# Reordering ScalarE's and VectorE's work in a two-layer hybrid mixer backbone

## What is computed

```python
for l in range(DEPTH):
    mod = jnp.split((silu_c @ w_mod[l] + b_mod[l])[:, None, :], 6, axis=-1)
    u = modulate(rmsnorm(h, g_mix_pre[l]), mod[0], mod[1])
    # y = (sum over 4 branches of sigmoid(gates_i) * (branch_i(u) @ w_branch[i])) @ w_out
    #     branches: a windowed attention, b bidirectional mLSTM, c latent attention, d differential attention
    y, y_ctx = token_mixers(u, uc, w_in[l], ...)
    h = h + mod[2] * rmsnorm(y, g_mix_post[l])
    u = modulate(rmsnorm(h, g_ffn_pre[l]), mod[3], mod[4])
    h = h + mod[5] * rmsnorm(swiglu(u, w_gate_up[l], w_down[l]), g_ffn_post[l])
    # the context stream hc likewise, in the first layer
return h
```

## Time and profile before

| what | value |
|---|---|
| median of three runs | 3376.95 us (3375.93 to 3379.35) |
| the profiled execution's own time | 3375.98 us |
| its span, first to last instruction | 3374.2 us |
| mean granted clock of TensorE | 0.977 |
| HBM read, written | 273.9 MB, 33.3 MB |

### The profile page before, as it was taken

How to read it: one execution, slowest core, us unless ns; L and a number is a source line. 1 busy time by engine, 2 the same in 40 slices (tenths; PEclk the granted TensorE clock), 3 DMA queues, 4 the chain that set the end, 5 groups by cost and what they waited for, 6 DMA issues and landing times. The chain is left out here.

```text
span 3374.2 us, 47244 instructions
## 1 busy us (share of the span) xinstructions
PE 3200.8 (95%) x18520; PEld 2902.2 (86%) x18520; DVE 1713.8 (51%) x3183; ACT 1136.5 (34%) x1931; POOL 216.7 (6%) x170
## 2 busy tenths in 40 slices
PE   7999989999999989899999989999999999899998
PEld 4999988998899879899999988877787887788886
DVE  6644465424346865764222575545433578553334
ACT  3233234423322544312222432334433225432323
POOL 0001100100021011000000000010100110100000
PEclk9999999999999999899999989999999999999999
DMA  5511230221052023432222443141221421332333
GB/s 204 171 38 59 87 124 26 76 91 45 23 187 76 26 75 121 135 125 68 70 63 59 136 144 103 63 125 38 88 88 38 167 77 38 138 113 84 109 88 93
DMA packets 356826, 310.27 MB, mean 92 GB/s; under 512 B 40527, under 2 KB 335389, under 8 KB 355229
## 3 DMA queue, kind: packets, MB, share of 16 engines
q1 hardware_dynamic: 334478, 240.65, 23.0%
q10 hardware_dynamic: 22158, 67.03, 5.3%
HBM read 273.94 MB, written 33.29 MB: 91 GB/s over the span
## 5 line engine op out<-in xcount | busy, mean ns | idle before, releaser
L868 PE MATMUL ps<-u_hi,w_hi 128*128 128x384 f32 (+1 forms) x2080 | 604.7, 353 | 22.3 <-DVE u_lo L2439 8.5
L868 PE MATMUL ps<-u_lo,w_hi 128*128 128x384 f32 (+1 forms) x2080 | 598.8, 350 | 0.0
L868 PE MATMUL ps<-u_hi,w_lo 128*128 128x384 f32 (+1 forms) x2080 | 598.7, 350 | 0.0
L2051 DVE TENSOR_TENSOR w_lo<-w_raw,w_hi 128x2048 fp32r<-128x2048 f32 x129 | 297.2, 2304 | 345.7 <-ACT w_hi L1520 343.8
L868 PEld LDWEIGHTS ps<-u_hi,w_hi 128*128 128x128 f32 x2080 | 380.4, 190 | 45.9 <-issue 24.8
L868 PEld LDWEIGHTS ps<-u_hi,w_lo 128*128 128x128 f32 x2080 | 383.3, 190 | 19.2
L868 PEld LDWEIGHTS ps<-u_lo,w_hi 128*128 128x128 f32 x2080 | 383.6, 190 | 18.8
L1520 ACT ACTIVATE w_hi<-w_raw 128x2048 fp32r<-128x2048 f32 x129 | 246.1, 1908 | 213.8 <-issue 91.2
L1238 PE MATMUL ps<-u_hi,w_hi 128*128 128x384 f32 (+1 forms) x816 | 310.3, 380 | 4.5 <-ACT space L1818 3.5
L1238 PE MATMUL ps<-u_hi,w_lo 128*128 128x384 f32 (+1 forms) x816 | 296.0, 363 | 0.0
L1238 PE MATMUL ps<-u_lo,w_hi 128*128 128x384 f32 (+1 forms) x816 | 293.5, 360 | 0.0
(11 more groups left out here) (305 smaller groups left out, 5241.2 us busy)
## 6 DMA issues: line engine op xcount, KB each, us to landing
w_raw<-in_w_in SPq DMA_DIRECT2D x288, 256.0 KB, 4.0
space<-in_w_mod SPq DMA_DIRECT2D x48, 1024.0 KB, 5.2
w_raw<-in_w_gate_up SPq DMA_DIRECT2D x176, 256.0 KB, 3.7
w_raw<-in_w_down SPq DMA_DIRECT2D x114, 192.0 KB, 2.7
w_raw<-in_w_branch SPq DMA_DIRECT2D x64, 256.0 KB, 3.5
w_raw<-in_w_out SPq DMA_DIRECT2D x48, 256.0 KB, 3.6
m_scratch<-space ACTq DMA_DIRECT2D x3, 3072.0 KB, 10.2
space<-m_scratch ACTq DMA_DIRECT2D x3, 3072.0 KB, 10.6
```

Of the source, the lines that this page charges most:

```text
L868: last = nc.tensor.matmul(ps[:, 2 * (t % 2) + b, 0:a1 - a0], wv[w][:, k, j * P:(j + 1) * P], xx[:, k, a0:a1], start=(k == 0 and w == 0 and ...
L2051: V.tensor_tensor(w_lo[slot][:, :], w_raw[slot][:, :], w_hi[slot][:, :].bitcast(F32), ALU.subtract).then_inc(w_lo_done, 1)
```

## The change

It moves work and adds little. ScalarE copies three high parts of branch3 between the two units of weights. In the mLSTM preparation TensorE's cumulative sums go from behind tile 5 to behind tile 6, ScalarE's exponential and logarithm from tile 3 to tile 4. VectorE multiplies the first two output-gate tiles ahead of the weight split. At a seam's end the weight split goes ahead of the mean. A one-element Silu is added at the end of the two seams before up0. In the tail the residual comes back in one transfer, is turned by 128 tokens x 8 chunks after the last product, into the eight PSUM banks, and the output operation reads it there; the 8 copies by VectorE fall away, the first sums go ahead of the last three products, and the stores read contiguous rows. The three units at a_q go elsewhere: the first layer's d_q, then up0, take the next ones, the last three of the second layer ride behind units 3, 6 and 9 of its up0 (`sparse`); up0 is written out in both layers (`unrolled`).

```diff
 class Background:
+        self.sparse = False
+    def at(self, i):
+        unit = self.first + i
+        return (self.layer, unit) if unit < MOD_UNITS else (self.layer + 1, unit - MOD_UNITS)
     def behind(self, at):
+        if self.sparse:
+            return [at // 3 - 1] if at % 3 == 0 and 0 < at // 3 <= self.end - self.first else []
...
-    for at, name, l, first, end, tile in ((0, "misc", 0, 8, 15, 4), (0, "a_q", 0, 15, 18, 24), (0, "d_q", 0, 18, 24, 20),
-                                          (0, "up0", 1, 0, 11, 0), (1, "misc", 1, 11, 18, 4), (1, "d_q", 1, 18, 24, 20)):
+    for at, name, l, first, end, tile in ((0, "misc", 0, 8, 15, 4), (0, "d_q", 0, 15, 21, 20), (0, "up0", 0, 21, 32, 0),
+                                          (1, "misc", 1, 8, 15, 4), (1, "d_q", 1, 15, 21, 20),
+                                          (1, "up0", 1, 21, 24, 0)):
         background[starts[at, name]] = Background(l, first, end, 1, b0, tile)
+        for g in groups:
+            background[starts[at, name]].sparse = end - first <= sum(h.n for h in groups) // 3
+            g.unrolled = end > MOD_UNITS or end - first < sum(h.n for h in groups) - 1
@@ pairs
-    first = whole if g.name in SQUARED else 1 if peel or g.early else 0
+    first = whole if g.name in SQUARED or g.unrolled else 1 if peel or g.early else 0
@@ SyncE
-                             H_TOKEN[:, :, token_tile(t)]).then_inc(out_stored, 16)
+                sp.dma_start(out[0, t * P:(t + 1) * P, :], out_tile(t)).then_inc(out_stored, 16)
@@ TensorE, gemm_unit in down1 of the second layer
-                                if made and k == HALF // 2:
-                                    turn_h(made - 1)
                                 if made and k == HALF // 2 + 1:
                                     turn_y(made - 1)
-                                if made == KD - 1 and k == HALF - 1:
+                                if made == KD - 1 and k == HALF - 2:
                                     final_sums(False)
@@ TensorE, prepare_b
-                if made == 5:
+                if made == 6:
                     pe.wait_ge(lf_ready, l + 1)
@@ TensorE, gemm, behind the last product
-                    turn_h(KD - 1)
+                    turn_h(groups[-1], 0)
                     final_sums(True)
                     turn_y(KD - 1)
+                    for t in range(1, SEQ // P):
+                        turn_h(groups[-1], t)
+            def turn_h(g, t):
+                if t == 0:
+                    pe.wait_ge(h_back, 16)
+                if t == 1:
+                    made = g.t0 + KD - 1
+                    pe.wait_ge(acc_free[made % 2], made // 2 + 1)
+                if t == 2:
+                    pe.wait_ge(mean_ready, n.mean)
+                if t == 3:
+                    pe.wait_ge(y_token, KD)
+                for k in range(KD):
+                    at = k * P % BW
+                    last = nc.tensor.transpose(ps[:, 2 * t + k * P // BW, at:at + P], H_LAST[:, k, token_tile(t)],
+                                               ident[:, :])
                 last.then_inc(h_turned, 1)
@@ ScalarE, prepare_b
-                if made == 3:
+                if made == 4:
                     act.wait_ge(lf_abs, DEPTH + l + 1)
@@ ScalarE, gemm
-                    act.dma_start(space[:, 0:8, CTX], h_dram[:, :, CTX_LEN:CTX_LEN + CTX_LEN]).then_inc(h_back, 16)
-                    act.dma_start(H_LATE, h_dram[:, :, 2 * CTX_LEN:TOK]).then_inc(h_back, 16)
+                    act.dma_start(H_LAST, h_dram[:, :, LAT]).then_inc(h_back, 16)
+                    if g.name == "branch3":
+                        gemm_unit(g, 0, 0)
+                        merged_high(g, 0, 3)
+                        gemm_unit(g, 0, 1)
+                        continue
...
+                    merged_high(g, 3, KD - 1)
+                    split_unit(following, 1, None)
+                    merged_high(g, KD - 1, KD)
@@ ScalarE, close
+                if following.kind == "swiglu":
+                    own.did(A(warm[:, :], half_neg[:, :], ACT.Silu))
+                    own.wait()
@@ VectorE, gemm_unit
+                if g.name == "gates1_rest":
+                    output_gate(g.layer, 0, 2)
                 if not first or not (g.early or g.name.startswith("down")):
                     split(g, it, s)
...
-                        output_gate(g.layer, g.lat)
+                        output_gate(g.layer, 2, NT)
+                        output_low(g.layer, g.lat)
...
-                        if k:
-                            h_copy(k - 1)
@@ VectorE, close
+                split(following, 0, 0)
                 part_mean(g, 1, h_sums, 2 * e + 2, next_mean)
-                split(following, 0, 0)
@@ VectorE, finish_output
-                h_copy(KD - 1)
...
                 for i in range(SEQ // P):
+                    dve.wait_ge(h_turned, i + 1)
+                    V.scalar_tensor_tensor(out_tile(i).rearrange("p (k n) -> p k n", k=KD), Y_TOKEN[:, :, token_tile(i)],
                                            root[:, CT + i:CT + i + 1],
-                                           H_TOKEN[:, :, token_tile(i)], ALU.mult,
+                                           ps[:, 2 * i:2 * i + 2, :].rearrange("p b (k n) -> p (b k) n", n=P), ALU.mult,
                                            ALU.add).then_inc(out_made, 1)
```

More of the change, by code:

```diff
@@ L72, in __init__ @@
         self.x, self.kind, self.dst = x, kind, dst
-        self.last = self.early = False
+        self.last = self.early = self.unrolled = False
         self.halves = 1 if lat else 2
@@ L97, in __init__, with stretches @@
         self.layer, self.first, self.end, self.per, self.b0, self.tile = layer, first, end, per, b0, tile
+        self.sparse = False
+    def at(self, i):
+        unit = self.first + i
+        return (self.layer, unit) if unit < MOD_UNITS else (self.layer + 1, unit - MOD_UNITS)
+    def stretches(self):
+        if self.end <= MOD_UNITS:
+            return [(self.layer, self.first, self.end)]
+        return [(self.layer, self.first, MOD_UNITS), (self.layer + 1, 0, self.end - MOD_UNITS)]
     def behind(self, at):
+        if self.sparse:
+            return [at // 3 - 1] if at % 3 == 0 and 0 < at // 3 <= self.end - self.first else []
         return [i for i in range(self.per * at, self.per * (at + 1)) if i < self.end - self.first]
     def rest(self, weight_units):
+        if self.sparse:
+            return range(0)
         return range(min(self.per * weight_units, self.end - self.first), self.end - self.first)
@@ L682, in load_back @@
                 slot = (bk.b0 + i) % 2
+                if isinstance(it, int):
+                    layer, unit = bk.at(i + 2 * bk.per * it)
+                    at = unit * 256
+                else:
+                    layer, at = bk.layer, (bk.first + i) * 256 + it * bk.per * 512
                 sp.dma_start(back_raw(bk, slot).rearrange("p (k n) -> p k n", k=KD),
-                             mod_cols(bk.layer, (bk.first + i) * 256 + it * bk.per * 512)).then_inc(
-                                 back_landed[slot], 16)
+                             mod_cols(layer, at)).then_inc(back_landed[slot], 16)
             def load_unit(g, it, s):
@@ L798, in unit @@
                             load_unit(g, it, s)
-                        if bk is not None and isinstance(it, int) and g.u0 - groups[0].u0 + s + 2 * it == 1:
+                        if bk is not None and isinstance(it, int) and g.u0 - groups[0].u0 + s + 2 * it == (3 if bk.sparse else 1):
                             sp.wait_ge(others_end, 3 * index)
@@ L856, in back_unit @@
                 pe.wait_ge(back_summed, bk.b0 + i + 1 + 2 * bk.per * it)
+                at = 4 * bk.at(i + 2 * bk.per * it)[1] if isinstance(it, int) else 4 * (bk.first + i) + 8 * bk.per * it
                 for j in range(2):
[L858 removed]
+                    last = part_product(back_part(bk, (bk.b0 + i) % 2), j, at)
                 last.then_inc(back_used, 1)
@@ L1141, in gemm @@
                 if groups[-1].name in SQUARED:
-                    turn_h(KD - 1)
+                    turn_h(groups[-1], 0)
                     final_sums(True)
                     turn_y(KD - 1)
-            def turn_h(k):
-                if not k:
-                    pe.wait_ge(h_back, 32)
-                if k:
-                    pe.wait_ge(h_token, k)
-                for t in range(SEQ // P):
-                    src = space[:, k, token_tile(t)] if t < CT else H_LATE[:, k, token_tile(t - CT)]
-                    last = nc.tensor.transpose(ps[:, 5, token_tile(t)], src, ident[:, :])
+                    for t in range(1, SEQ // P):
[14 more added lines that the diff above has]
+                                               ident[:, :])
                 last.then_inc(h_turned, 1)
@@ L1627, in y_copy, with merged_high @@
                 A(Y_TOKEN[:, k, :], ps[:, 6, :], ACT.Copy).then_inc(y_token, 1)
+            def merged_high(g, first, end):
```

(18 more changed lines are left out.)

20 lines of the change are left out of this document (9 added, 11 removed).

## The result

The changed kernel took 3344.49 us in the median (3343.54 to 3346.87, four runs), the kernel before 3378.15 on the same chip: ratio 0.9893, 95% interval 0.988 to 0.9907, so 1.07% faster, where I forecast 1.7%. 3344.5 lies above my range (3306 to 3342). Run once more, beside the kernel before at 3380.55, it took 3339.99: ratio 0.9888 (0.9862 to 0.9914). The profiled execution took 3345.4 us, its span is 3343.7, its mean granted clock 0.979 (before 0.977).

What follows compares the result with a forecast made beforehand. TensorE, busy 95% of the span, was taken as the bound, so only its stalls and the low clock behind them count. Seven terms summed to 55.9 us, 18.8 of it clock: 3376.0 to 3320 us, 1.7% faster, range 3306 to 3342.

Steps and rivals of the forecast that it cites:

- a_q: First layer: modulation units leave this phase; 8.9 plus 0.6 of clock, less 2.7 in second-layer up0, net 6.8 us.
- mLSTM preparation: Later cumulative sums remove the log-gate waits and low clock: 3.4 us in the first layer, 5.7 in the second, together 9.1.
- Output gate: Two multiplies ahead of the w_lo split remove the third turn's waits and low clock: 4.5 + 6.1 = 10.6 us.
- branch1's first unit, over 10 us off: Output gate: what the delayed w_lo split holds up is wanted only there, more than 10 us later.
- branch3: Early high parts on ScalarE remove accumulator waits and low clock, less a new 1.4 us wait: 6.5 + 4.3 = 10.8.
- Norms: Three seams: splitting w_lo ahead of the mean shortens TensorE's wait for GpSimd's root; 5.8 us, no clock gain.
- Silu table: Start of up0, both layers: dummy activation hides the 1.28 us load and the clock stays up; 6.0 us.
- My sign of being wrong: A w_lo split or chunk sum as releaser in branch3 or up0, output operations over 1.3 us, or clock falling as often.
- Tail: End of down1: residual turns leave, its transfer wait and low clock go, first sums cost 1.0; 6.8 us gained.
- (a): Rival: stalls go but the clock does not come back, 3339 us; chance 0.15, half of it lying in between.
- (b): Rival: VectorE becomes the pace in branch3 and in up0's three units, 3330 us; chance 0.12.
- the likeliest case: All seven terms hold, giving 3320 us; chance 0.59.

Runs made afterwards that it cites:

- e8: Changed kernel with the 4-byte tile warm allocated behind all other tiles instead of ahead of the large ones; 3334.65 us, ratio 0.9854.
- e9: Kernel before with one unused 4-byte tile, moving the large tiles by 32 bytes; 3389.66 us, ratio 1.0027.
- e4: Changed kernel with the mLSTM preparation put back, cumulative sums, exponential and logarithm one tile earlier; 3351.34 us, ratio 0.9919.
- e13: e11 with the output gate as before, all multiplies behind VectorE's w_lo split; 3333.14 us, 6.1 over e11.
- e1: Changed kernel with the chunk sums behind the gate product in the first unit of the first layer's up0; 3331.55 us, ratio 0.9856.
- e2: Changed kernel without the dummy Silu that loads the table early; 3335.40 us, ratio 0.9868.
- e7: Kernel before with only the dummy Silu added at the end of the seams that lead into up0; 3389.47 us, ratio 1.0023.
- e16: Kernel before with one unused tile of 256 bytes, moving the large tiles by 256 bytes; 3380.42 us, ratio 0.9995.
- e0: The changed kernel run and profiled once more, nothing altered; 3339.99 us, ratio 0.9888.
- e11: Changed kernel with three repairs: warm behind all tiles, late chunk sums in first-layer up0, residual's load after the third tile; 3327.02 us, ratio 0.9838.
- e6: Changed kernel with late chunk sums in first-layer up0 and the residual's load after the third tile, warm not moved; 3329.50 us, ratio 0.9848.
- e3: Changed kernel with the residual's load in the seams behind w_out issued after the third tile instead of the seventh; 3333.52 us, ratio 0.9867.
- e10: Kernel before with one unused tile of 64 bytes, moving the large tiles by 64 bytes; 3385.69 us, ratio 1.0012.
- e15: Kernel before with one unused tile of 128 bytes, moving the large tiles by 128 bytes; 3385.91 us, ratio 1.0021.

## Why the prediction was off, point by point

**What bounds the kernel: right.** TensorE's busy time didn't move (3200.8 to 3199.2), and all gain came from its waits and its clock.

**a_q: right as a term.** 9.4, 8.8 for a sum of 9.5, and 2.7 for the units in up0 of the second layer (-1.1 is the 2.7 less the 1.7 of clock that I had booked there). The wait in front of prep_a is 1.73 instead of 3.55, and the clock behind is 0.54 for 0.61, so that it fell as far behind the shorter stall:

```profile
458.98 0.44 PE L1255 MATMUL ps<-ident,space 128*128 128x128 f32 x2 [1.73 <-DVEq L490]
```

What I missed is d_q: it takes other units than before, and TensorE's wait there is 0.9 with the old distribution and unmoved tiles, 1.7 with the new one, 1.9 with the old and moved ones, 2.9 with both (before, e8, e9, the changed kernel). Why the distribution costs 0.8 was not tried.

**mLSTM preparation: right in the second layer**, 6.2 for 5.7 by TensorE's own products: the wait for r_in is 0.3 where I said 0.8. In the first layer the wait of 1.7 is gone, but the gain of 3.4 isn't shown, neither by the start-up row nor by e4.

**Output gate: right in the first layer (4.6 for 4.5), 1.9 too high in the second.** The step that failed is "branch1's first unit, over 10 us off". The low parts of y now stand behind the split, and TensorE waits 0.9 for one. It also waits 0.9 for an accumulator, and e13 shows that this one isn't the reordering's: it comes with the old order too. The trace before has none there, and it had lost 3.4 us to the low clock just ahead of that place; that the slower TensorE was its cover is likely and not shown:

```profile
PE ps L900 <- DVEq L2182: 0.9, 1, 0.9
PE ps L900 <- DVE y_lo L2209: 0.9, 1, 0.9
```

**branch3: right**, 7.0 and 3.6 for 6.5 and 4.3, with VectorE's pace of 1.77 us beside GpSimd, and a new wait of 1.4, as forecast:

```profile
2871.57 1.77 DVE L2192 TENSOR_TENSOR u_lo<-space,u_hi 128x512 fp32r<-128x512 f32 x1
2873.27 0.67 DVE L2176 TENSOR_TENSOR space<-space,ps 128x512 f32<-128x512 f32 x1
2874.09 1.77 DVE L2192 TENSOR_TENSOR u_lo<-space,u_hi 128x512 fp32r<-128x512 f32 x1
```

**Norms: the wait is right** (11.0 to 5.1, forecast 5.8). One of the twelve roots is long still, beside the w_lo split of L2322, not on the path:

```profile
L2909 POOL TENSOR_TENSOR root<-mean,half_neg x12: 696/850/2826, 1299.7 to 2960.5; 128x3 f32<-128x3 f32 x8, 128x2 f32<-128x2 f32 x4
```

**Silu table: this step failed.** "The dummy activation hides it ... and the clock should stay" holds in the second layer (2.20 to 0.92, and 1.7 of clock). In the first it gained 0 of 3.0 and 1.2 went besides, 4.2 in all. I followed the wait that was removed and not the one behind it: the trace before has, eleven microseconds on, a wait of 0.88 for the gate product, which said that another chain, transfer, sums, product, was nearly as late. TensorE at the lower clock was cover for it. Taking 1.28 and 1.7 away, with the unit landing later, made it 4.2, and this stall brought a fallen clock of its own. e1, e2 and e7 show it. So does e16, the kernel before with only a tile more: there the clock didn't fall behind the first wait, and the second is 2.4. The rows of the kernel before, then of e16:

```profile
PE ps L868 <- DVEq L2082: 0.9, 1, 0.9
```

```profile
PE ps L869 <- DVEq L2083: 2.4, 1, 2.4
```

That stage is 1.6 us longer in e16 than in the first profile, so the 1.2 that "went besides" can be the base's luck; the 3.0 wasn't there to be had in either. My sign of being wrong, a chunk sum in up0, had come true, though the releaser named is the product behind the sums.

**Tail: too low by 1.5.** 8.3 to 8.5 for 6.8. The output operations take 4.86 us with their operand in PSUM, as with it in SBUF (4.87), the bound that I took at nothing; the end after them is 4.05 us instead of 4.6, and down1's tiles are 0.5 shorter each.

**Not in the sum at all: the addresses. This step failed too.** I costed `warm` as one activation and its place in memory at nothing, without a reason. It costs 9.3 us by e9 (5.7 to 12.8 by its interval), 5.3 by e8 against e0, 2.5 by e11 against e6. No row of the kernel before could price it, but that an allocation ahead of the large tiles moves them was there to be read in the kernel.

**The base.** The sum was made against 3376.0. In six comparisons the kernel before had medians of 3378 to 3381, so that its profile was a quick one. Up to 220 us it lost 10.2 us to the low clock, the changed kernel 17.1 and 18.8 in its two samples, e3 8.5, e16 18.8. It falls otherwise from trace to trace of kernels that are the same there. What decides it stays open.

**The 25.4 us that are missing** in the first profile lie, by the table, in the second layer's last seam (9.8, which e0 mostly doesn't have), the start-up (5.9), up0 of the first layer (4.2), the stretch to branch3 in the second layer (3.4), its output gate (1.9) and behind up0 (1.7); single rows came out a little better or worse. Of these up0 and part of the stretch to branch3 are explained by experiments, the last seam goes with the late transfer (in e3, e6 and e11, which load it early, that stage gained 2.9 to 3.7); the start-up isn't explained.

The rivals: (a), the clock that doesn't come back, is what the first total mostly looks like: only 6.4 of the 18.8 us came back (78.4 to 72.0), 11.0 in the second trace and 16.8 in e11. But at the places of the removed stalls it did come back in the second layer's preparation, the gates, branch3 and the tail, and what took its place was the start-up, the late transfers and up0. (b) came true only as far as my sum had it. Of the seven terms of the likeliest case four held, the preparation's held in one layer and isn't shown in the other, the gate's was 1.9 too high, the Silu's failed; and one cost, the addresses, had no term.

## What to carry to other kernels

- Before booking a removed wait, look for the next wait of the same engine and ask which chain ends it. If that chain doesn't start at the removed one, the gain stops at the slack between them, and the lower clock inside it was slack too.
- A new tile, however small, belongs behind the large ones, or the tiles that transfers write must be put back to a multiple of 256 bytes. It is one line to try: an unused tile in the kernel before.
- A change made of many small reorderings can be checked stage by stage, by the starts of one repeated instruction in both traces. The total has an uncertainty of 7 us here, most stages of 1.7, one low stretch more or less, and a start-up or a seam of more. Profile the kernel before more than once, or a loss may be the first profile's luck.

## What the runs showed of the hardware

- Transfers from HBM ran at 385 GB/s into tiles at a multiple of 256 bytes, and at 349 into tiles 32 bytes past one (d_q, second layer); 32, 64 and 128 bytes past all ran at 346 to 354 (e9, e10, e15), 256 bytes past at 383 to 388 (e16).
- The fallen clock is not in proportion to the stall: 0.54 for 6 us behind a stall of 1.73 (the changed kernel's prep_a), none behind one of 2.20 (e2, second layer), where before one of 2.20 had it.
- A transfer of 3 MB took 10.2, 10.3 and 12.5 us to land at the same place of the program. With the one of 12.5 (the changed kernel's first trace) went a wait of 3.0, a clock of 0.54 in both windows read in the seam, and 9.3 us in that stage against e0.
